# A two-layer hybrid trunk on one core: input projection, convolution taps and attention scores in another order

## The chip, the core and the metric

The kernel runs on one core of a Trainium2 chip. The metric is the time of one execution on the device in microseconds (us). The engines are named as in the profile: PE is the matrix engine (TensorE), DVE the vector engine, ACT the scalar engine, POOL GpSimd, and SP the engine from whose queue the weights are loaded. Every engine runs its own instructions in order; semaphores join them.

## What is computed

Two layers over x of 256 tokens by 1024 channels in float32. In each layer one input projection feeds a convolution module and a sparse attention, whose results are joined by one output projection; then comes a dense SwiGLU (layer 0) or a top-2-of-8 expert SwiGLU (layer 1).

```python
for layer in range(DEPTH):
    h = rms_norm(x, attn_norm_g[layer])
    z = h @ w_in[layer]
    c_val, c_gate, q, k_c, v_c, k_s, v_s, k_w, v_w, g_log = jnp.split(z, offsets, axis=-1)
    conv_out = conv_module(c_val, c_gate, ...)      # GLU, causal 31-tap depthwise conv, norm of 64 channels, silu
    attn_out = nsa_attention(q, k_c, v_c, ...)
    x = x + jnp.concatenate([conv_out, attn_out], axis=-1) @ w_out[layer]
    h = rms_norm(x, ffn_norm_g[layer])
    x = x + (swiglu(h, ...) if layer % 2 == 0 else moe_swiglu(h, ...))
```

The attention has 8 query heads of 64 in 2 key/value heads. Queries and keys are normalised per head. The compressed branch attends to 15 blocks of 32 keys, each put through a small two-layer network (cmp_k_w1, cmp_v_w1 and so on); the selected and the window branch attend, at 256 tokens, to all keys before the query under a causal mask. Three gates per head weigh the branches.

## The kernel before

**Storage.** Weights come into one ring of four slots of 2 MB (`stream` sets the order, SP loads them, and a load waits on `last_read` of what stood in its slot). In the dense and expert stages the same ring is cut into seven pieces of 1 MB. Activations of the attention live in `arena`, `hn` and `mixT`. PSUM has eight banks. The profile calls `arena` what the code calls z, qT, kT, u, y, probsT and more, so lines tell them apart.

**The stretch ahead of the attention,** in each layer. PE multiplies the normalised, transposed input `hT` with: `z_product(0, i)` (keys and values of the compressed branch and others, 512 columns, for two token tiles i), four gated chunks c (`glu(c)`, 128 channels of value and gate each, from weight chunks `win` 0 and 1), then the compression products of keys and values (L1137, weights `cmp` 0 and 1), `z_product(1, i)` (queries) and `z_product(2, i)` (keys and values of the window branch and the gate logits), with small transposes between them. DVE applies the 31 taps (`conv_taps`, L737 for the first tap and L741 for the others, one instruction per tap and chunk): first chunks 0 and 1, then 2 and 3. A chunk pair can begin when both `glu` of it are there. Between the taps DVE squares, sums and normalises queries and keys (L776 to L821) and finishes their transposes (L827, L831). The order of taps and the rest is written out by hand (`TAP_A`, `TAP_B`, `TAP_C`); the last 12 taps of chunks 2 and 3, 24 instructions, stand behind `masked_scores(1)`.

**The attention core.** There are 12 units of scores (4 heads by 128 keys for the first token tile, 2 heads by 256 keys for the second). For unit n: PE `score(n)` (L1186) writes bank n % 2; DVE adds the causal mask into `hn` (L841) and takes the negated maximum (L843); ACT exponentiates per head (L516); DVE divides by the sum and multiplies by the gate (L882 to L886); PE transposes (`transpose_probs`, L1212); ACT copies the result (L540); after the last unit of a group of heads PE multiplies with the values (`values`, L1223 and L1227). In the loop PE issues score(n+2), which waits until DVE has read unit n (`s_ready`), then the transposes of unit n. Ahead of the loop stand score(0), score(1), the compressed scores (L1200, 16 products of 15 columns), their softmax on DVE (L855 to L873) behind the last taps, and the transposes of it (L1235), whose copies by ACT (L531) PE waits for. The means and variances of the convolution (L1247, L1253) are multiplied in the loop at n = 1 and n = 5. Then follows the output projection (L1268).

**The dense stage.** For group g of 256 hidden channels (11 groups): `up` (L1288 to L1290) for w1 and w3, `down(g - 1)` (L1304 to L1306). All operands are split in a high and a low part in fp32r. `dact_hi` (ACT, L583) and `dact_lo` (DVE, L918) hold the activation of one group: writing group g - 1 waits for the products of group g - 2.

## Time and profile before

| | us |
|---|---|
| median of 3 runs | 1653.21 (1651.16 to 1655.38) |
| the profiled execution | 1654.8 |
| span of its core | 1652.8 |
| PE busy | 1563.0 (95%) |
| DVE busy | 1211.1 (73%) |
| ACT busy | 911.5 (55%) |
| mean granted clock of PE | 0.957 |

The profile's page has busy shares in 40 slices of 41.3 us, the chain of work that ended last, and the costliest groups of instructions. A row of the chain is: start, duration, engine, what it writes, line. A row of the timeline is: start, duration, engine, line, operation, out<-in, shapes, count, and in brackets how long the engine sat idle before it and who ended that. A busy PE is not PE at its peak. A float32 matmul or its weight load appears twice in the timeline of PE for one product of the program, a transpose and an fp32r matmul once.

### The profile page before, as it was taken

How to read it: one execution, taken by the hardware profiler on the slowest of the kernel's cores; microseconds unless marked ns; L12 is line 12 of the kernel's file. 1: busy time of each engine (PE TensorE's matmuls, PEld its weight loads, DVE VectorE, ACT ScalarE, POOL GpSimd, SP SyncE). 2: the span in 40 equal slices, each digit the busy share in tenths (PEclk: the TensorE clock that was granted, in tenths of full speed). 3: DMA queues.
4: the chain of work that ended last, by engine and by line, in shares of the span. 5: the costliest groups of instructions: out<-in, count | busy, mean ns of one | idle time of the engine just before them, and what ended most of it. 6: DMA issues, size and time to landing. Idle time of an engine off the chain costs nothing.

```text
span 1652.8 us, 19780 instructions
## 1 busy us (share of the span) xinstructions
PE 1563.0 (95%) x7336; PEld 1233.4 (75%) x7336; DVE 1211.1 (73%) x1186; ACT 911.5 (55%) x834; POOL 24.3 (1%) x41
## 2 busy tenths in 40 slices
PE   6968899998896888999999999999999999999998
PEld 4654389998665437888888888888888888888886
DVE  2876254453287624888987988987988987989896
ACT  1024233432102424677777777777777677777674
POOL 1010000000001000000000000000000000000000
PEclk9977899999997788999999999999999999999999
DMA  8500086541551003999999999999999998999992
GB/s 291 180 2 1 0 286 205 189 161 53 202 181 51 1 0 136 356 367 371 361 359 332 365 368 371 361 359 334 361 371 372 360 365 328 359 372 365 363 364 102
DMA packets 199396, 426.57 MB, mean 258 GB/s; under 512 B 7314, under 2 KB 40338, under 8 KB 199316
## 3 DMA queue, kind: packets, MB, share of 16 engines
q1 hardware_dynamic: 198000, 424.89, 71.4%
q8 instruction: 64, 1.05, 0.3%
q10 hardware_dynamic: 1316, 0.49, 0.1%
q14 instruction: 16, 0.13, 0.0%
HBM read 424.31 MB, written 1.05 MB: 257 GB/s over the span
## 4 chain that ended last, share of the span: by engine, by line
PE 89%; DVE 7%; issue 2%; ACT 2%; DMA 1%; ACTq 0%; POOL 0%; POOLq 0%; DVEq 0%
PE bank L1387 13%; PE bank L1389 12%; PE bank L1388 12%; PE bank L1094 8%; PE bank L1411 6%; PE bank L1409 6%; PE bank L1410 6%; PE bank L1290 3%; PE bank L1289 3%; PE bank L1288 3%; PE bank L1268 3%; PE bank L1227 2%; PE bank L1137 2%; PE bank L1397 1%; PE bank L1186 1%
## 5 line engine op out<-in xcount | busy, mean ns | idle before, releaser
L717 DVE TENSOR_TENSOR w_lo<-ring,w_hi 128x2048 fp32r<-128x2048 f32 x369 | 843.1, 2291 | 184.3 <-ACT w_hi L471 183.8
L471 ACT CAST w_hi<-ring 128x2048 fp32r<-128x2048 f32 x369 | 705.4, 1914 | 268.3 <-PE bank L1389 165.3
L1387 PE MATMUL bank<-w_hi,xe_hi 128*128 128x512 f32 x896 | 355.2, 396 | 7.4 <-DVE w_lo L717 7.4
L1389 PE MATMUL bank<-w_hi,xe_lo 128*128 128x512 f32 x896 | 350.1, 391 | 0.0
L1388 PE MATMUL bank<-w_lo,xe_hi 128*128 128x512 f32 x896 | 349.7, 390 | 0.0
L1387 PEld LDWEIGHTS bank<-w_hi,xe_hi 128*128 128x128 f32 x896 | 168.7, 188 | 43.0 <-DVE w_lo L717 9.6
L1389 PEld LDWEIGHTS bank<-w_hi,xe_lo 128*128 128x128 f32 x896 | 168.6, 188 | 35.9
L1388 PEld LDWEIGHTS bank<-w_lo,xe_hi 128*128 128x128 f32 x896 | 168.9, 188 | 33.2
L1409 PE MATMUL bank<-w_hi,actT_hi 128*128 128x512 f32 x448 | 175.1, 391 | 0.0
L1410 PE MATMUL bank<-w_lo,actT_hi 128*128 128x512 f32 x448 | 174.5, 389 | 0.0
L1411 PE MATMUL bank<-w_hi,actT_lo 128*128 128x512 f32 x448 | 174.4, 389 | 0.0
L1288 PE MATMUL bank<-hT_hi,w_hi 128*128 128x256 f32 x352 | 99.6, 283 | 0.0
L1290 PE MATMUL bank<-hT_hi,w_lo 128*128 128x256 f32 x352 | 99.6, 283 | 0.0
L1289 PE MATMUL bank<-hT_lo,w_hi 128*128 128x256 f32 x352 | 99.6, 283 | 0.0
L1411 PEld LDWEIGHTS bank<-w_hi,actT_lo 128*128 128x128 f32 x448 | 84.1, 188 | 17.6
L1409 PEld LDWEIGHTS bank<-w_hi,actT_hi 128*128 128x128 f32 x448 | 84.1, 188 | 17.0
L1410 PEld LDWEIGHTS bank<-w_lo,actT_hi 128*128 128x128 f32 x448 | 84.1, 188 | 17.0
L741 DVE SCALAR_TENSOR_TENSOR arena<-arena,par 128x256 f32<-128x256 f32 x240 | 96.1, 477 | 0.0
L712 DVE TENSOR_TENSOR x_sb<-x_sb,bank 128x512 f32<-128x512 f32 x48 | 30.6, 683 | 67.9 <-PE bank L1268 58.7
L1094 PE MATMUL bank<-ring,hT 128*128 128x512 f32 (+1 forms) x192 | 74.4, 543 | 3.2 <-DVE hT L705 3.2
L1289 PEld LDWEIGHTS bank<-hT_lo,w_hi 128*128 128x128 f32 x352 | 67.5, 192 | 0.4
L1288 PEld LDWEIGHTS bank<-hT_hi,w_hi 128*128 128x128 f32 x352 | 67.5, 192 | 0.4
(224 smaller groups left out, 1472.7 us busy)
## 6 DMA issues: line engine op xcount, KB each, us to landing
ring<-in_moe_w SPq DMA_DIRECT2D x336, 1024.0 KB, 6.1
ring<-in_dense_w SPq DMA_DIRECT2D x33, 1024.0 KB, 5.4
ring<-in_w_in SPq DMA_DIRECT2D x8, 2048.0 KB, 10.3
ring<-in_w_out SPq DMA_DIRECT2D x4, 2048.0 KB, 9.0
ring<-in_cmp_k_w SPq DMA_DIRECT2D x2, 2048.0 KB, 19.2
ring<-in_cmp_v_w SPq DMA_DIRECT2D x2, 2048.0 KB, 8.7
ring<-in_w_in SPq DMA_DIRECT2D x2, 1120.0 KB, 11.4
x_sb<-in_x SPq DMA_DIRECT2D x2, 512.0 KB, 5.1
```

The costliest lines, as they stand in the source:

```text
L471: nc.scalar.copy(w_hi[t % SPLIT][:], raw(t)).then_inc(w_hi_ready, 1)
L717: V.tensor_tensor(w_lo[t % SPLIT][:], raw(t), w_hi[t % SPLIT][:].bitcast(F32), ALU.subtract).then_inc(w_lo_ready, 1)
L1094: last = T.matmul(dst, lhs(k), rhs(k), start=(n == 0), stop=(n == len(chunks) - 1))
L1288: T.matmul(dst, hi[:, k, c], hT_hi[:, k, :], start=(k == 0), stop=False)
L1289: T.matmul(dst, hi[:, k, c], hT_lo[:, k, :], start=False, stop=False)
L1290: last = T.matmul(dst, lo[:, k, c], hT_hi[:, k, :], start=False, stop=(k == KD - 1))
L1387: T.matmul(dst, xe_hi[:, kk, own], hi[:, k, :], start=(kk == 0), stop=False)
L1388: T.matmul(dst, xe_hi[:, kk, own], lo[:, k, :], start=False, stop=False)
L1389: last = T.matmul(dst, xe_lo[:, kk, own], hi[:, k, :], start=False, stop=(kk == KD - 1))
L1409: T.matmul(dst, actT_hi[:, c % 2, f], hi[:, k, r], start=first, stop=False)
L1410: T.matmul(dst, actT_hi[:, c % 2, f], lo[:, k, r], start=False, stop=False)
L1411: last = T.matmul(dst, actT_lo[:, c % 2, f], hi[:, k, r], start=False, stop=end)
```

## The change

1. Loads: `win` 0 and 1 come first and in halves of 256 columns. The first halves of both (chunks 0 and 1) signal `glu_arrived[0]`, the second halves `glu_arrived[1]`. `win` 3 comes third. The load of the compression weights of the values now takes over the slot of `win` 0 and waits for the fourth gated chunk.
2. PE makes chunks 0 and 1 first, then `z_product(0, i)`, chunk 2, the transposes for the compression, chunk 3.
3. DVE's taps are placed anew: all 124 stand ahead of the first `masked_scores`.
4. Queries and keys are normalised, transposed and finished per token tile, one part earlier; kT is transposed in two parts.
5. The compressed keys `kcT` are laid out block-diagonally (zeroed at the start by GpSimd), so that 8 products of 64 columns replace 16 of 15, in one bank, ahead of the last key transposes. Their softmax takes fewer, wider instructions. It stands on DVE between `masked_scores(0)` and `masked_scores(1)` and behind the first unit's probabilities; its transposes come at n = 1 of the loop and not ahead of it.
6. The causal mask enters the bank by one fp32r matmul (`ident_r` by `causal_r`, 512 columns) ahead of each unit's scores, which accumulate on it. DVE's add (L841) is gone; the maximum and ACT's exponentials read PSUM. Score(n+2) now waits for unit n's exponentials (`exp_ready`).
7. `dact_hi` and `dact_lo` have two buffers.
8. The means of the convolution are multiplied at n = 2.

DVE around the first scores of a layer. Before:

```order
L741 SCALAR_TENSOR_TENSOR arena<-arena,par 128x256 x6
L821 TENSOR_TENSOR hn<-arena,rstat 128x128 x2
L827 TENSOR_SCALAR arena<-bank0,par 128x4x128
L827 TENSOR_SCALAR arena<-bank1,par 128x4x128
L831 TENSOR_SCALAR arena<-bank2,par 128x256 x2
L841 TENSOR_TENSOR hn<-bank0,causal 128x512
L843 TENSOR_REDUCE negmax<-hn 128x4
L841 TENSOR_TENSOR hn<-bank1,causal 128x512
L843 TENSOR_REDUCE negmax<-hn 128x4
L741 SCALAR_TENSOR_TENSOR arena<-arena,par 128x256 x24
L855 TENSOR_TENSOR cp<-bank6,cneg 128x4x15 x2
```

The same place of the changed kernel, where L757 are the taps, L814 and L819 finish queries and keys, L866 is the maximum, and L908 the first unit's probabilities:

```order
L814 TENSOR_SCALAR arena<-bank7,par 128x4x128
L847 TENSOR_TENSOR arena<-arena 128x128 x2
L848 TENSOR_REDUCE stat<-arena 128x4
L849 TENSOR_SCALAR stat<-stat 128x4
L814 TENSOR_SCALAR arena<-bank5,par 128x4x128
L819 TENSOR_SCALAR arena<-bank2,par 128x256
L854 TENSOR_TENSOR hn<-arena,rstat 128x128 x2
L757 SCALAR_TENSOR_TENSOR arena<-arena,par 128x256 x4
L819 TENSOR_SCALAR arena<-bank3,par 128x256
L866 TENSOR_REDUCE negmax<-bank0 128x4
L875 TENSOR_TENSOR cp<-bank6,cneg 128x16x15
L876 TENSOR_REDUCE cmx<-cp 128x16
```

No tap stands between the first scores and the compressed softmax any more, and four stand shortly before the first scores.

PE from the first score of a layer to the loop. Before, with the transposes of the compressed probabilities (L1235) ahead of the third unit's scores:

```order
L1186 MATMUL bank0<-arena 128x128 x4
L1186 MATMUL bank1<-arena 128x128 x4
L1200 MATMUL bank6<-kcT,arena 128x15 x8
L1200 MATMUL bank7<-kcT,arena 128x15 x8
L1235 MATMUL bank6<-ident,cp 64x128 x4
L1235 MATMUL bank7<-ident,cp 64x128 x4
L1186 MATMUL bank0<-arena 128x128 x4
L1212 MATMUL bank2<-ident,hn 128x128 x4
L1186 MATMUL bank1<-arena 128x128 x4
L1212 MATMUL bank3<-ident,hn 128x128 x4
```

Now (L1217 compressed scores, L1228 mask, L1232 scores, L1249 transposes of probabilities, L1273 those of the compressed ones):

```order
L1217 MATMUL bank6<-kcT,arena 128x64 x8
L1199 MATMUL bank3<-ident,hn 128x128 x2
L1228 MATMUL bank0<-causal_r,ident_r 128x512
L1232 MATMUL bank0<-arena 128x128 x4
L1228 MATMUL bank1<-causal_r,ident_r 128x512
L1232 MATMUL bank1<-arena 128x128 x4
L1228 MATMUL bank0<-causal_r,ident_r 128x512
L1232 MATMUL bank0<-arena 128x128 x4
L1249 MATMUL bank2<-ident,hn 128x128 x4
L1228 MATMUL bank1<-causal_r,ident_r 128x512
L1232 MATMUL bank1<-arena 128x128 x4
L1249 MATMUL bank3<-ident,hn 128x128 x4
```

The compressed scores moved ahead of the first scores, and their transposes (L1273, the next rows) behind the second unit's.

The loads that SP issues for layer 0, before:

```order
L347 DMA ring<-in_w_in 128x8x512 x3
L347 DMA ring<-in_cmp_k_w 128x16x256
L347 DMA ring<-in_cmp_v_w 128x16x256 [waits z_psum]
L347 DMA ring<-in_w_in 128x8x512 [waits glu_psum]
L347 DMA ring<-in_w_in 128x8x280 [waits glu_psum]
```

And now:

```order
L353 DMA ring<-in_w_in 128x8x256 x2
L356 DMA ring<-in_w_in 128x8x256 x2
L359 DMA ring<-in_w_in 128x8x512
L359 DMA ring<-in_cmp_k_w 128x16x256
L359 DMA ring<-in_cmp_v_w 128x16x256 [waits glu_psum]
L359 DMA ring<-in_w_in 128x8x512 [waits glu_psum]
```

The load of `cmp_v_w` moved from behind `z_product(0)` to behind the last gated chunk.

The core of the diff:

```diff
-        stream += [("win", l, 3), ("win", l, 0), ("win", l, 1), ("cmp", l, 0), ("cmp", l, 1), ("win", l, 2), ("win", l, 4)]
+        stream += [("win", l, 0), ("win", l, 1), ("win", l, 3), ("cmp", l, 0), ("cmp", l, 1), ("win", l, 2), ("win", l, 4)]
...
-                sp.dma_start(dst[:, 0:k * m].rearrange("p (k n) -> p k n", k=k), src).then_inc(arrived, 16)
+                dst = dst[:, 0:k * m].rearrange("p (k n) -> p k n", k=k)
+                if key in halved:
+                    sp.dma_start(dst[:, :, 0:S], src[:, :, 0:S]).then_inc(glu_arrived[0], 16)
+                    if key[2] == 1:
+                        for c in range(2):
+                            sp.dma_start(view("win", key[1], c)[:, :, S:BANK],
+                                         source("win", key[1], c)[0][:, :, S:BANK]).then_inc(glu_arrived[1], 16)
+                else:
+                    sp.dma_start(dst, src).then_inc(arrived, 16)
...
-                            if g >= 2:
-                                sc.wait_ge(w_used, piece_of["d2", 0, g - 2] + 1)
-                            nc.scalar.copy(dact_hi[:].rearrange("p a t -> p (a t)"),
+                            if g >= 3:
+                                sc.wait_ge(w_used, piece_of["d2", 0, g - 3] + 1)
+                            nc.scalar.copy(dact_hi[:, (g - 1) % 2].rearrange("p a t -> p (a t)"),
...
                 link(V.memset(blkT[:], 0.0))
+                glu(0)
+                glu(1)
+                dv.wait_ge(u_ready, CC * l + 2)
+                conv_taps(0, range(16))
                 for i in range(NT):
                     dv.wait_ge(z_ready, 6 * l + i + 1)
...
-                glu(0)
+                conv_taps(0, range(16, 23))
+                glu(2)
...
-                glu(1)
-                dv.wait_ge(u_ready, CC * l + 2)
-                conv_taps(0, range(6))
-                glu(2)
-                conv_taps(0, range(6, 15))
+                conv_taps(0, range(23, TAPS))
                 glu(3)
-                conv_taps(0, range(15, TAPS))
...
-                conv_taps(2, range(TAP_A))
+                conv_taps(2, range(22))
                 square_sums_q(0)
-                conv_taps(2, range(TAP_A, TAP_B))
+                conv_taps(2, range(22, 26))
+                normalised_q(0)
...
-                    s3 = scores[:, n % 2, :].rearrange("p (h k) -> p h k", h=nh)
-                    link(V.tensor_tensor(s3, bank[n % 2][:].rearrange("p (h k) -> p h k", h=nh),
-                                         causal[:, 2 * P - keys:].unsqueeze(1).to_broadcast([P, nh, keys]), ALU.add))
-                    V.tensor_reduce(negmax[:, n % 2, 0:nh], s3, AX_X, ALU.max, negate=True).then_inc(s_ready, 1)
+                    V.tensor_reduce(negmax[:, n % 2, 0:nh], bank[n % 2][:].rearrange("p (h k) -> p h k", h=nh),
+                                    AX_X, ALU.max, negate=True).then_inc(s_ready, 1)
...
                 masked_scores(0)
+                compressed_scores()
                 masked_scores(1)
-                conv_taps(2, range(TAP_C, TAPS))
...
+                    if n == 0:
+                        compressed_probs()
-                    if n == 2:
+                    if n == 3:
...
                     if n >= 2:
-                        pe.wait_ge(s_ready, NU * l + n - 1)
+                        pe.wait_ge(exp_ready, exp_count(l, n - 2))
                     r = slice(kv * HD, (kv + 1) * HD)
+                    T.matmul(bank[n % 2][:], ident_r[:],
+                             causal_r[:, 2 * P - keys:].unsqueeze(1).to_broadcast([P, nh, keys]),
+                             start=True, stop=False)
                     for h in range(nh):
                         last = T.matmul(bank[n % 2][:, h * keys:(h + 1) * keys], qT[r, h0 + h, i * P:(i + 1) * P],
-                                        kT[r, b, 0:keys], start=True, stop=True)
+                                        kT[r, b, 0:keys], start=False, stop=(h == nh - 1))
```

## Rows read from the trace of the kernel before

**Rows 1.** The page: granted clock in 40 slices, in tenths, then the chain's engines.
```profile
PEclk9977899999997788999999999999999999999999
PE 89%; DVE 7%; issue 2%; ACT 2%; DMA 1%; ACTq 0%; POOL 0%; POOLq 0%; DVEq 0%
```

**Rows 2.** Chain of waits, layer 0's attention core, from the first scores on.
```profile
105.67 3.79 PE bank L1186 x16
...
110.90 9.50 DVE arena L741 x24
...
125.17 1.93 PE bank L1235 x8
127.13 1.07 ACT arena L531 x2
128.24 2.07 PE bank L1186 x8
...
141.68 1.07 PE bank L1186 x4
```

**Rows 3.** Chain of waits, layer 1: first scores, output projection.
```profile
518.54 3.79 PE bank L1186 x16
...
599.20 13.95 PE bank L1268 x32
```

**Rows 4.** Windows: busy and count by engine, granted clock, DMA share, GB/s; in the core.
```profile
112.00:116.00 4.00, 3.26 (x20) 3.15 (x18) 4.00 (x12) 0.58 (x4) 0.00 (x0) 0.50 0.01 2
152.00:156.00 4.00, 4.00 (x16) 2.15 (x15) 3.79 (x9) 2.37 (x8) 0.00 (x0) 1.00 0.00 0
180.00:184.00 4.00, 4.00 (x6) 0.98 (x5) 0.00 (x0) 2.44 (x5) 0.00 (x0) 0.50 0.00 0
```

**Rows 5.** Timeline of the stretch ahead: compression products, then DVE's wait for queries.
```profile
67.79 7.11 PE L1137 MATMUL bank<-ring,arena 128*47 128x256 f32 x32
83.17 0.69 DVE L776 TENSOR_TENSOR arena<-arena 128x512 f32<-128x512 f32 x1 [0.25 <-ACT arena L482]
99.75 1.09 PE L1170 MATMUL bank<-ident,hn 128*128 128x128 f32 x8 [0.48 <-ACT arena L482]
```

**Rows 6.** The page: one load, its size, us from issue to landing.
```profile
ring<-in_cmp_v_w SPq DMA_DIRECT2D x2, 2048.0 KB, 8.7
```

**Rows 7.** Timeline of the core: one unit's pieces, and values at either clock.
```profile
130.24 1.12 PE L1212 MATMUL bank<-ident,hn 128*128 128x128 f32 x4
137.21 0.69 DVE L892 TENSOR_TENSOR arena<-arena,bank 128x512 f32<-128x512 f32 x1 [0.37 <-PE bank L1247]
139.75 1.93 PE L1227 MATMUL bank<-arena 128*64 128x512 f32 x4
164.58 6.58 PE L1227 MATMUL bank<-arena 128*64 128x512 f32 x8
186.14 27.73 PE L1268 MATMUL bank<-ring,mixT 128*128 128x512 f32 x64
```

**Rows 8.** Groups by line and shape over 0 to 225 us: busy, mean ns.
```profile
L843 DVE TENSOR_REDUCE negmax<-hn 128x4 f32<-128x512 f32 x4 | 2.7, 686 | 0.1
L516 ACT ACTIVATE hn<-hn,negmax 128x256 f32<-128x256 f32 x16 | 8.0, 500 | 3.1 <-DVE negmax L843 3.0
```

**Rows 9.** Chain of waits in the expert stage: fp32r matmuls of 512 columns.
```profile
661.47 0.43 PE bank L1387
...
662.25 0.23 PE bank L1389
```

**Rows 10.** Timeline of the end of the dense stage.
```profile
401.49 0.69 DVE L927 TENSOR_TENSOR dact<-dsg,bank 128x512 f32<-128x512 f32 x1 [6.78 <-PE bank L1290]
...
406.94 0.62 ACT L583 CAST dact_hi<-dact 128x512 fp32r<-128x512 f32 x1 [10.68 <-PE bank L1306]
411.73 0.79 PE L1304 MATMUL bank<-w_hi,dact_hi 128*128 128x512 f32 x1 [4.89 <-DVE w_lo L717]
```

**Rows 11.** A window in which PE ran transposes alone (L1086, L1075).
```profile
427.00:428.00 1.00, 1.00 (x12) 1.00 (x11) 1.00 (x2) 0.00 (x0) 0.00 (x0) 1.00 1.09 345
```

More of the change, by code:

```diff
@@ L78, in hymba_trunk @@
     slot_of = {key: n for n, key in enumerate(slots)}
+    halved = [key for key in slots if key[0] == "win" and key[2] < 2]
+    turn_of = {key: len([o for o in slots[:n + 1] if o not in halved and slot_of[o] % SLOTS == n % SLOTS])
+               for n, key in enumerate(slots)}
     piece_of = {key: n for n, key in enumerate(pieces)}
@@ L207, in hymba_trunk @@
         x_loaded, par_loaded = sem("x_loaded"), sem("par_loaded")
+        glu_arrived = [sem(f"glu{h}_arrived") for h in range(2)]
         slot_arrived = [sem(f"slot{s}_arrived") for s in range(SLOTS)]
@@ L1192, in _ @@
                 score(1)
-                pe.wait_ge(kcT_ready, l + 1)
-                pe.wait_ge(vc_ready, l + 1)
-                for kv in range(KV):
-                    r = slice(kv * HD, (kv + 1) * HD)
-                    for i in range(NT):
-                        for g in range(G):
-                            o = (i * G + g) * CPAD
-                            last = T.matmul(bank[6 + kv][:, o:o + NCMP], qT[r, g, i * P:(i + 1) * P],
-                                            kcT[r, kv * CPAD:kv * CPAD + NCMP], start=True, stop=True)
-                    last.then_inc(cs_psum, 1)
                 def transpose_probs(n):
@@ L1303, in down @@
                                     dst, r = bank[2 * n + i][:], slice(i * P, (i + 1) * P)
[L1304 to L1306 removed]
+                                    T.matmul(dst, dact_hi[:, g % 2, f, r], hi[:, f, c], start=first, stop=False)
+                                    T.matmul(dst, dact_hi[:, g % 2, f, r], lo[:, f, c], start=False, stop=False)
+                                    last = T.matmul(dst, dact_lo[:, g % 2, f, r], hi[:, f, c], start=False, stop=end)
                         last.then_inc(w_used, 1)
```

204 lines of the change are left out of this document (116 added, 88 removed).

## The prediction

> **What bounds the kernel now.** I read the page first. PE stands for 89% of the chain and its clock is granted in full in most of the 40 slices; it drops in three places, slices 3 to 4, slice 10 and slices 13 to 15 [rows 1]. Those are the attention core of layer 0, the end of the dense stage and the core of layer 1. Between them PE works without a gap worth naming, and nothing that the change touches runs in the expert stage after about 650 us. So the chain of waits is read next, in those places only.
>
> In layer 0 the first scores start at 105.67 and the output projection at 186.14 [rows 2, 7]: a core of 80.5 us. In layer 1 it is 518.54 to 599.20, 80.7 us, with the same pieces [rows 3]. In both, PE has made two units of scores and the compressed scores and then waits for DVE, which works through 24 taps (9.5 us) and the compressed softmax: PE's next instruction, the transposes at 125.17, comes ten microseconds after its last [rows 2]. After that the loop of 12 units alternates between a full clock and half of it: 1.00 at 152 to 156, 0.50 at 112 to 116 and at 180 to 184 [rows 4]. Four value products cost 1.93 at the one and eight cost 6.58 at the other, 0.46 against 0.82 each [rows 7]. The third place is one wait: the last `down` of the dense stage starts 4.89 us late, because ACT could only write `dact_hi` once PE had read the last one [rows 10].
>
> **Part 1: the stretch ahead of the scores.** The products are the same, in another order, and PE stays the bound if DVE keeps up. From the first gated pair (about 31) to the scores (106) DVE has 74 us. Its work there is 124 taps at 9.50/24 = 0.40 [rows 2], 49 us, and some 18 us of other steps that it had before: 67. The closest point is the squares of the queries, for which DVE waited 0.25 us before [rows 5]. With the new order, laid one step after the other behind their gated chunks (glu 0 and 1 by 32; 30 taps and two first taps to 45; 14 to 52; the compression input 4 us; 16 to 64; 44 to 81.5) DVE is there at 81.5, and the queries come at about 84. So 2.8 us of cover; beyond that every microsecond would count.
>
> Two things are added on PE's path. The load of the compression weights of the values is issued only when chunk 3 is done, at 60.2, and takes 8.7 us [rows 6]; PE wants them at 67.79 [rows 5], so it waits 60.25 + 8.7 - 67.8 = 1.1. And four transposes of queries (half of the 1.09 for eight [rows 5]) now stand ahead of the last projection product: 0.55. Behind that product, the way to the first score took 105.67 - 99.75 = 5.9 [rows 2, 5]. Of it two taps go (0.8) and one 512-column finish (0.7), since one token tile's queries are done earlier; one more round between PE and DVE for the second half of the keys costs some 0.3: 4.7. The compressed scores fit into PE's wait there. Sum: 1.1 + 0.55 - 1.2 = +0.4 for each layer. At the start of layer 0 the halved loads bring rows of 1 KB; even at the 2 MB in 8.7 us of rows 6 the first 2 MB land ahead of 16 us, when PE starts. Bounds of this part: -0.5 (no wait for the load) to +3 (load 2 us later, DVE's cover used up).
>
> **Part 2: the core up to the fourth unit.** Before: first score to the head of n = 3 (the score at 141.6), 35.9 us [rows 2]. Now, with a unit's scores at 1.07 (8 instructions at half clock: 2.07) [rows 2], and the mask's matmul, which the trace before does not have in this place: its nearest row is an fp32r matmul of 512 columns, 0.23 at full clock, 0.43 at half [rows 9]. At full clock: units 0 and 1 until 2.6; maximum 0.72 [rows 8] and four exponentials 2.3, until 4.5; score(2) and the transposes of unit 0 until 6.5. ACT does unit 1 until 6.8 and the compressed exponential until 7.3; DVE the compressed rest (2.2), the maximum of unit 2 (0.7) and the probabilities of unit 1 (1.1) until 11.4; PE its transposes (0.6) and the compressed ones (1.1) until 13.1; two copies by ACT as in rows 2, until 14.4; score(4), transposes (0.59, half of the 1.12 at low clock [rows 7]), means (4 instructions of 512 columns, 1.75) and values (6 of them, 2.65, by the 0.46 of rows 7 or a little less) until 20.7. At half clock the same list ends at about 30; half clock up to the means and full behind gives 26.5. PE has holes of 2 to 3 us here, so I take the clock low until unit 3, nearly: 25.5. The gain is 35.9 - 25.5 = 10.4: the 9.5 us of taps, moved under the projections, and about one more.
>
> **Part 3: units 3 to 11.** Before: 186.14 - 141.6 = 44.5. PE's work at full clock now: 7 scores at 1.07 + 0.23 = 9.1, 9 transposes at 0.59 = 5.3, variances 1.75, values 2.65 + 2 x 4.35 = 11.35: 27.5. Its waits: the mask's 0.7 on DVE is gone from each unit, but score(n+2) now comes behind unit n's exponentials (two at 0.50 + 0.1 each [rows 8], 1.35), side by side with DVE's probabilities (1.1). Where values stand in between this hides; in the last four units it does not, and following exponential, score, maximum, exponential I get 7.1 us of waits. That makes 34.6 at full clock throughout. With the last value products at half clock, as at 180 to 184, +4.4; with those of the third group too, another +4. I take 39: the holes of over a microsecond ahead of the last values are still there. The same list for the units before, with the clock of its rows, comes out some 2 us long, which is within this choice. Gain 44.5 - 39 = 5.5. ACT reading PSUM instead of SBUF I cost at nothing, bounds -1.5 to +1.5 for the core.
>
> A core then takes 64.5 instead of 80.5. The Trainium skill (TensorE: Matmul & The Clock Gate, Part 4) says that transposes don't count as busy for the clock. By that the clock would stay low here. The trace disagrees: at 427 to 428 only transposes ran and the granted clock was 1.00, after 0.50 before them [rows 11].
>
> **Part 4: the dense stage.** From the start of `dact_hi` to PE's start it was 411.73 - 406.94 = 4.8, the splitting of the last weights by ACT and DVE. With two buffers `dact_hi` can be written when DVE's product is there, at 402.2 [rows 10]: PE starts at 402.2 + 4.8 + 0.2 = 407.2 instead of 411.73, -4.5. After the wait of 4.9 the clock was at half for the first ten matmuls or so, 0.43 instead of 0.23 [rows 9]; with a wait of 0.6 that should go, -2.2, bounds 0 and -2.4. In the other groups PE did not wait, so nothing changes there.
>
> **Sum.** Two layers x (0.4 - 10.4 - 5.5) = -31.0; dense -6.7; together -37.7. 1654.8 - 37.7 = 1617.1 against the profiled execution, which is 1.6 above the median: **1615.5**. The copies of the mask and the clearing of kcT lie in the first 7 us, when ACT and GpSimd wait for x.
>
> **The rivals.**
> (a) The clock stays at full speed in the core, because the mask's matmuls fill PE: 20.7 + 34.6 = 55.3 per core, 9.2 less each: 1615.5 - 18.4 = 1597. For it: each unit has more columns than before; against it: PE still stands still for 2 to 3 us at four places.
> (b) DVE or the load decides ahead of the scores: the cover of 2.8 us is gone and the load comes 2 us later; +2.6 per layer, +5: about 1621. For it: DVE is now busy for 67 of 74 us.
> (c) The lost lookahead costs more: score(n+2) behind the exponentials serialises every unit, also those that I let hide behind values. 1.3 us for 7 units and the third value group at half clock, 10 less 3 of it already counted, so +6 per core: about 1628.
> (d) Slower than before: the clock stays at half through the whole core, as it did from 104 to 136. PE's list at half clock is 77 us of work, with waits 83.5, and the output projection, which began at full clock, loses 2. Per layer 83.5 + 0.4 + 2 - 80.5 = +5.4, two layers 10.8, dense only -4.5: +6.3, 1659.5. It decides from a core of over 82 us. Against it: the full clock came back three times in the old loop, with less work in it. The rule of the Trainium skill that is named above points here.
> (e) The change doesn't do what it says: the taps do fill the time ahead, but PE then waits there as long as it did behind; the gain of part 2 is nil. That is 1636. DVE's idle time in the stretch ahead speaks against it.
>
> **Chances.** Forecast (1608 to 1619) 50%; (a) 13%; (b) 16%; (c) 13%; (d) 3%; (e) 5%. The range leaves out the lower half of (a), (d) and (e): 1602 to 1630. About 0.3%, 5 us, is what a measurement can tell from no change. Faster 0.95, the same 0.02, slower 0.03.
>
> **What would show it.** In the profile after: no taps behind the first maximum; the first scores of layer 0 at 105 to 107; from there to the output projection 60 to 69 us; a wait of about a microsecond at the second compression product; the last `down` of the dense stage less than a microsecond behind the one before, at full clock; the distance from the output projection of layer 1 to the end as before. A core of under 58 us makes (a) right, one over 70 (c). If the expert stage itself gets longer or shorter, the sum was made in the wrong place.

## The result, and the profile after

| | us |
|---|---|
| before, median of 20 runs | 1654.48 (1650.40 to 1656.76) |
| changed kernel, median of 20 runs | 1642.07 (1634.67 to 1658.54) |
| ratio | 0.9928, 95% interval 0.9915 to 0.9942 |
| profiled execution after: span | 1641.6 |
| the same, PE busy, clock | 1586.6 (97%), 0.97 |

The change gains 12 us, not the 38 that were predicted, and the time lies above the predicted range. The sign was right, the size was not.

The page after, busy time of the engines, then the granted clock in 40 slices (the counterpart of [rows 1]):

```profile
PE 1586.6 (97%) x7328; PEld 1227.3 (75%) x7328; DVE 1194.1 (73%) x1156; ACT 908.1 (55%) x834; POOL 24.0 (1%) x42
...
PEclk9978999999997799999999999999999999999999
```

The clock's two drops below 9 are shorter, two slices each instead of three and four. (The prediction counted three drops and named slice 10; [rows 1] has a 9 there. The clock does fall at the end of the dense stage, to 0.50 at 412 to 416, but too briefly to bring that slice below 9.) But PE is busy for 23.6 us more than before (1563.0) in a kernel that is shorter and in which its waits shrank. That is the first sign that its work got slower somewhere.

The chain of waits after, start and duration, from layer 0 to the first expert product; it answers to [rows 2, 3]. L1228 is the first mask, L1309 the output projection, L1428 the first expert product:

```profile
59.03 8.37 DMA ring<-in_cmp_v_w
67.44 7.11 PE bank L1163 x32
...
104.53 0.76 PE bank L1228
...
130.58 0.43 PE bank L1228
...
170.81 19.51 PE bank L1309 x45
```
```profile
395.57 1.29 DVE x_sb L729 x2
449.43 9.29 DMA ring<-in_cmp_v_w
458.77 8.79 PE bank L1163 x32
...
497.77 0.76 PE bank L1228
565.24 13.95 PE bank L1309 x32
623.36 0.80 PE bank L1428
```

In the kernel before, the last dense products ended at 419.63 and the expert products began at 658.57:

```profile
419.63 0.69 DVE x_sb L712
...
658.57 0.77 PE bank L1387
```

Laid side by side, every difference has a place:

| stretch | before | after | difference | predicted |
|---|---|---|---|---|
| start to the first scores, layer 0 | 105.67 | 104.53 | -1.1 | +0.4 |
| core, layer 0 | 80.5 | 66.3 | -14.2 | -15.9 |
| output projection to the end of the dense stage | 233.5 | 224.8 | -8.7 | -6.7 |
| from there to the first scores of layer 1 | 98.9 | 102.2 | +3.3 | +0.4 |
| core, layer 1 | 80.7 | 67.5 | -13.2 | -15.9 |
| output projection to the first expert product | 59.4 | 58.1 | -1.3 | 0 |
| expert stage | 994.2 | 1018.2 | +24.0 | 0 |

Up to the expert stage the changed kernel is 35.2 us ahead (37.7 predicted). Then it loses 24 in a stage in which no instruction was changed. Two windows of 25 us in it, before and after, columns as in [rows 4]; PE does nothing but matmuls of 512 columns in both, with no idle time and at a granted clock of 1.00:

```profile
733.00:758.00 25.00, 25.00 (x114) 20.71 (x113) 22.41 (x14) 18.28 (x12) 0.00 (x0) 1.00 1.02 374
```
```profile
733.00:758.00 25.00, 25.00 (x111) 20.14 (x110) 22.28 (x15) 19.14 (x16) 0.00 (x0) 1.00 1.01 365
```

114 matmuls against 111 in the same time, those under way at the edges counted. The timeline of PE shows the pace of one, if one takes starts and not durations (the matmuls overlap). Before, six starts lie 1.36 us apart, 0.227 each; after, 1.40, 0.233:

```profile
733.00 0.39 PE L1388 MATMUL bank<-w_lo,xe_hi 128*128 128x512 f32 x1
...
734.36 0.39 PE L1388 MATMUL bank<-w_lo,xe_hi 128*128 128x512 f32 x1
```
```profile
732.85 0.39 PE L1428 MATMUL bank<-w_hi,xe_hi 128*128 128x512 f32 x1
...
734.25 0.39 PE L1428 MATMUL bank<-w_hi,xe_hi 128*128 128x512 f32 x1
```

Over the whole stage the mean from start to start is 0.2272 before and 0.2332 after. There are 4032 such matmuls: 4032 x 0.0060 = 24 us, all of the loss. The page says it in one row for each kernel (mean duration 396 against 402 ns), and its idle time has not grown, so nothing is waited for:

```profile
L1387 PE MATMUL bank<-w_hi,xe_hi 128*128 128x512 f32 x896 | 355.2, 396 | 7.4 <-DVE w_lo L717 7.4
```
```profile
L1428 PE MATMUL bank<-w_hi,xe_hi 128*128 128x512 f32 x896 | 360.6, 402 | 6.8 <-DVE w_lo L734 6.8
```

### The profile page after: what moved, and what is told of

The parts are those of the page before. It is cut to its first block, busy times and chain, and to the rows that moved or that the text cites. A ratio compares the mean times of both kernels' runs of the same rounds, so it can differ in the third digit from the quotient of the medians.

```text
span 1641.6 us, 19740 instructions
## 1 busy us (share of the span) xinstructions
PE 1586.6 (97%) x7328; PEld 1227.3 (75%) x7328; DVE 1194.1 (73%) x1156; ACT 908.1 (55%) x834; POOL 24.0 (1%) x42
## 4 chain that ended last, share of the span: by engine, by line
PE 91%; DVE 4%; issue 2%; ACT 2%; DMA 1%; POOL 0%; ACTq 0%; POOLq 0%; DVEq 0%; SPq 0%
PE bank L1428 13%; PE bank L1430 13%; PE bank L1429 13%; PE bank L1120 8%; PE bank L1450 6%; PE bank L1452 6%; PE bank L1451 6%; PE bank L1309 3%; PE bank L1329 3%; PE bank L1331 3%; PE bank L1330 2%; PE bank L1264 2%; PE bank L1438 1%; PE bank L1345 1%; PE bank L1347 1%
## 5 line engine op out<-in xcount | busy, mean ns | idle before, releaser
L1428 PE MATMUL bank<-w_hi,xe_hi 128*128 128x512 f32 x896 | 360.6, 402 | 6.8 <-DVE w_lo L734 6.8
L1429 PE MATMUL bank<-w_lo,xe_hi 128*128 128x512 f32 x896 | 355.0, 396 | 0.0
L1430 PE MATMUL bank<-w_hi,xe_lo 128*128 128x512 f32 x896 | 354.9, 396 | 0.0
L1428 PEld LDWEIGHTS bank<-w_hi,xe_hi 128*128 128x128 f32 x896 | 169.0, 189 | 46.6 <-DVE w_lo L734 8.4
L757 DVE SCALAR_TENSOR_TENSOR arena<-arena,par 128x256 f32<-128x256 f32 x240 | 96.2, 480 | 0.1
```

The source lines that it names most:

```text
L1428: T.matmul(dst, xe_hi[:, kk, own], hi[:, k, :], start=(kk == 0), stop=False)
L1429: T.matmul(dst, xe_hi[:, kk, own], lo[:, k, :], start=False, stop=False)
L1430: last = T.matmul(dst, xe_lo[:, kk, own], hi[:, k, :], start=False, stop=(kk == KD - 1))
```

## What made the expert stage slower

**The theory.** Three tensors of the change stand in SBUF ahead of the activations of the dense and the expert stage: `kcT` grew from 47 to 64 columns (64 bytes more per partition, with the rounding of its place), `ident_r` (512 bytes) and `causal_r` (1024 bytes) are new. So the room of the attention's `mixT` and `arena`, and with it `hT_hi`, `dact_hi`, `xe_hi`, `actT_hi`, which use the same room later, moved by 1600 bytes, while the weights `w_hi` and `w_lo` stand ahead of all of them and stayed. Theory A: the pace of a matmul depends on where its operands lie. (The operand that is loaded into PE is called stationary, in the expert products the activations; the other, there the weights, is streamed through and called moving.) Rivals: the new instructions leave something behind that slows PE, or the loads or the copies by ACT and DVE, which now fall at other moments, collide with it.

**e1 and e2** move the activations of the kernel before and change nothing else, by an unused tensor behind `vc`: 400 columns (1600 bytes) and 16 (64 bytes).

```diff
+        gap = sb("gap", [P, 400])     # e2: 16, e3: 32
```

> The kernel before, with an unused tensor of 1600 bytes per partition ahead of the activation areas, so that these stand where they stand in the changed kernel; no instruction changes. The changed kernel reached the output projection of layer 1 some 33 us earlier than before, but its expert stage took 22.8 us longer (1017 against 994 us), with fp32r matmuls 0.2334 us apart instead of 0.2278 on average. Theory A (placement: the pace of the matmuls depends on where the stationary operands stand): this kernel is slower than before by 20 to 25 us, all of it in the expert stage, with 0.233 us between matmuls. Theory B (the earlier start or another order of events brings the loads or the engines into another rhythm): the same time as before within 3 us and 0.228 us.

> The kernel before with the activation areas shifted by 64 bytes per partition only. Theory A1 (placement, and what counts is whether an area starts at a multiple of 128 bytes): 20 to 25 us slower than before, as with a shift of 1600. Theory A2 (placement, but the distance of 1600 bytes or the crossing of a larger boundary counts): the same as before within 3 us. Theory B: the same as before within 3 us.

> The kernel before with the activation areas shifted by 128 bytes. Theory A1: the same as before within 3 us. Theory A2 leaves it open: between 0 and +23 us. Theory B: the same as before within 3 us.

> The changed kernel with the activation areas shifted by another 64 bytes, to a multiple of 128. Theory A1: the expert stage goes back to about 994 us and the time to 1619 us, 34 us under before. Theory A2: 1642 us, as the changed kernel. Theory B: 1642 us.

Measured: e1 1676.31 us, ratio to before 1.0124 (1.0101 to 1.0147); e2 1676.83, 1.0127 (1.0106 to 1.0148). Both have 0.2332 us for each expert matmul. An empty tensor alone costs the kernel before 20 to 21 us: the new instructions, the loads and the waits are out, and 64 bytes do what 1600 do (1600 = 6 x 256 + 64). The loss lies where it lay in the changed kernel, in the expert stage: 1016.6 us in both traces against 994.2 before. The page's row of e2:

```profile
L1387 PE MATMUL bank<-w_hi,xe_hi 128*128 128x512 f32 x896 | 360.0, 402 | 6.4 <-DVE w_lo L717 6.4
```

e3 (128 bytes) took 1673.74, 1.0109 (1.0086 to 1.0132), with 0.2324, and e4, the changed kernel with 64 bytes more, 1639.52, 0.9897 (0.9857 to 0.9937), with 0.2325. So 128 bytes are no better a place than 64, or hardly. The idea that any multiple of 128 would do fell.

**e5** moves the two areas of the changed kernel on until they are 2048 bytes from where they stood before, **e6** places the expert stage's two groups apart: `h_hi` to `xe_lo` at 128 modulo 512, `actT_hi` and what follows at 384. (`w_hi` is placed at byte 82048 of each partition, which is 128 modulo 512; `xe_hi` at 187776 before, 189376 in the changed kernel and 189824 in e5, so 0, 64 and 0 from it modulo 256.) **e7** moves weights and activations of the kernel before together by 64 bytes.

```diff
-        hT_hi, hT_lo = sb_d("hT_hi", [P, KD, S], F32R), sb_d("hT_lo", [P, KD, S], F32R)
+        gap_d = sb_d("gap_d", [P, 112]); hT_hi, hT_lo = sb_d("hT_hi", [P, KD, S], F32R), sb_d("hT_lo", [P, KD, S], F32R)
...
-        h_hi, h_lo = sb_e("h_hi", [P, NT, D], F32R), sb_e("h_lo", [P, NT, D], F32R)
+        gap_e = sb_e("gap_e", [P, 112]); h_hi, h_lo = sb_e("h_hi", [P, NT, D], F32R), sb_e("h_lo", [P, NT, D], F32R)
```

> The changed kernel with 448 unused bytes ahead of the activations of the dense stage and of those of the expert stage, so that both start 2048 bytes behind their place in the kernel before, at the same place within 512 bytes (384). So far, by the place within 512 bytes: 384 gave 0.2272 us between fp32r matmuls of 512 columns, 448 gave 0.2332, 0 gave 0.2324. Theory A3 (the pace goes by the place of the stationary operands within 512 bytes or a part of them): 0.2272 in the expert stage, which takes 994 us again, and 1619 us in all. Theory A4 (the kernel before stood at the one good distance from the weights by chance): 0.232 to 0.233 and 1640 us.

> The changed kernel with the gathered inputs of the experts (stationary in L1428 to L1430) at 128 within 512 bytes and their hidden activations (stationary in L1450 to L1452) at 384. Theory A3: the second group is paced at 0.2272; the first too if only the place within 256 bytes counts, 0.232 to 0.233 if it is within 512. Theory A4: both at 0.232 to 0.233. The time follows: 1619, 1634 or 1640 us, as two thirds of the matmuls are of the first group.

> The kernel before with 64 unused bytes behind the raw weights: the split weights, which move, and the stationary activations both stand 64 bytes further, their distance unchanged. If the distance of the two operands sets the pace: 0.2272 and the time of before within 3 us. If the place of the stationary operand alone does: 0.2332 and 20 us slower than before, as with 64 bytes ahead of the activations only.

e5: **1619.93 us**, ratio 0.9795 (0.9773 to 0.9818), 22.1 less than the changed kernel. Its row, again with 396 ns:

```profile
L1428 PE MATMUL bank<-w_hi,xe_hi 128*128 128x512 f32 x896 | 355.0, 396 | 7.8 <-DVE w_lo L734 7.8
```

e6: 1619.49, 0.9781 (0.9750 to 0.9812), both groups at 0.2273, while its dense stage, left where the change had put it, kept 0.2333. So the places repeat every 256 bytes, each product goes by its own operands, and nothing is left behind from one stage to the next. e7: 1654.47, 0.9997 (0.9984 to 1.0009), at 0.2273: with both operands moved, nothing happens. It is the distance between them that counts, not the place.

One rival is left: ACT and DVE write the weights that PE reads, so the distance could set how they collide with PE. A stretch in which neither of them works rules it out. At the end of the dense stage, first before, then after:

```profile
417.00:419.00 2.00, 2.00 (x11) 1.63 (x10) 0.00 (x0) 0.00 (x0) 0.00 (x0) 1.00 1.05 393
```
```profile
390.00:395.00 5.00, 5.00 (x23) 4.04 (x22) 0.00 (x0) 0.00 (x0) 0.00 (x0) 1.00 0.88 277
```

The 512-column products start 0.228 apart in the first (417.15 to 419.20, nine steps) and 0.233 in the second (390.95 to 395.15, 18 steps). The loads, which go on there, write into `ring`; e2 and e7 move the activations equally far from it, and only e2 is slower. So the cause of the loss is the distance of PE's two operands; why it acts so, no run shows.

## What the parts of the change are worth

From here the kernel with the repaired layout (e5) is the base, so that the core can be measured without the expert stage. Only the dense part was done alone, on the kernel before.

**e8**: two buffers for `dact_hi` and `dact_lo`, nothing else.

> The kernel before with the two buffers of the dense activations alone; nothing moves within 512 bytes. The step of the prediction: PE starts the last down 4.5 us earlier and at full clock, 6.7 us less, 1648 against 1655. Rival: the wait goes but the gain is lost behind it, since the next layer's weights or the additions to x come last: 0 to 3 us.

1645.64 us, 0.9945 (0.9925 to 0.9964): -9 us, with an interval of 6 to 12, where 6.7 was predicted. In the trace the dense stage, from the output projection on, takes 226.63 us and not 233.45: -6.8. The rival (0 to 3 us) fell. DVE's last steps of the dense stage in e8, then PE's first `down` behind them. Against [rows 10] the wait of 4.89 is gone, the first matmul starts at 406.32 instead of 411.73, and none runs at 0.43:

```profile
400.78 0.69 DVE L927 TENSOR_TENSOR dact<-dsg,bank 128x512 f32<-128x512 f32 x1 [7.30 <-PE bank L1290]
...
403.97 2.29 DVE L717 TENSOR_TENSOR w_lo<-ring,w_hi 128x2048 fp32r<-128x2048 f32 x1 [1.12 <-ACT w_hi L471]
```
```profile
406.32 0.50 PE bank L1304
406.82 0.23 PE bank L1305
```

**e9** puts 24 taps back behind the second unit's maximum, **e10** puts the mask and the wait of score(n+2) back on DVE, **e11** loads the compression weights of the values into the slot of `win` 3, which is free earlier, **e12** is e11 with `hT_hi` and `hT_lo` at 64 modulo 256 from the weights and `dact_hi`, `dact_lo` at 0. These four ran on one chip and e5 on another, so they are best compared by their ratios to the kernel before, which ran beside each.

```diff
-                conv_taps(2, range(22))
+                conv_taps(2, range(19))
...
                 masked_scores(1)
+                conv_taps(2, range(19, TAPS))
```
```diff
-                        pe.wait_ge(exp_ready, exp_count(l, n - 2))
+                        pe.wait_ge(s_ready, NU * l + n - 1)
...
-                    T.matmul(bank[n % 2][:], ident_r[:],
-                             causal_r[:, 2 * P - keys:].unsqueeze(1).to_broadcast([P, nh, keys]),
-                             start=True, stop=False)
...
+                    link(V.tensor_tensor(s3, bank[n % 2][:].rearrange("p (h k) -> p h k", h=nh),
+                                         causal[:, 2 * P - keys:].unsqueeze(1).to_broadcast([P, nh, keys]), ALU.add))
```
```diff
+    for l in range(L):
+        n = slot_of["win", l, 0]
+        slot_of["cmp", l, 1], slot_of["win", l, 2], slot_of["win", l, 4] = n + 6, n + 4, n + 5
+        slot_of["wout", l, 1] = n + 10
```
```diff
+        gap_d = sb_d("gap_d", [P, 48])
         dact_hi, dact_lo = sb_d("dact_hi", [P, 2, 2, S], F32R), sb_d("dact_lo", [P, 2, 2, S], F32R)
```

> The changed kernel with the repaired layout of e5 (1619.9 us), and in it one part of the change undone: the last 12 taps of chunks 2 and 3 (24 instructions) stand behind the second unit's maximum again, as in the kernel before. The prediction put the gain of their place at 9.5 of the 10.4 us of part 2 in each layer. Theory A (part 2 as told): DVE reaches the first unit's probabilities 24 x 0.40 = 9.5 us later and PE, which stands at their transposes, waits as long; a little comes back ahead of the scores, where four taps stood (0.8 per layer): +17 us, 1637. Rival B (PE had holes that the taps fill in part, and the new order of the compressed softmax hides some): +10 or less, 1630 or below. Rival C (rival (e) of the prediction, PE only waits elsewhere): no difference, 1620.

> The changed kernel with the repaired layout of e5 (1619.9 us), and in it the mask undone: DVE adds it into SBUF and takes the maximum there, the exponentials read SBUF, PE's 12 mask products per layer are gone, and score(n+2) waits for the maximum of unit n and no longer for its exponentials. Theory A (part 3 as told, the mask's addition gone from each unit weighs more than the lookahead): 0.69 us per unit come back on the path for 10 of 12 units, less the lookahead's gain, so +3 to +5 us per layer, +8 in all: 1628. Rival B (rival (c) of the prediction, the lost lookahead costs as much as the addition saved): no difference, 1618 to 1622. Rival C (the lookahead is worth more): faster by 4 us or more, 1616 or below.

> The changed kernel with the repaired layout of e5 (1619.9 us), and in it the compression weights of the values are loaded into the slot of win 3, which is free after z_product(0), and win 2 and win 4 into those of win 0 and win 1; the order of the loads stays. The load of the values' weights no longer waits for the fourth gated chunk. The trace of e5 shows PE waiting 0.82 us for this load in layer 0 and 2.15 us in layer 1, where the products behind it also run at a lower clock. Theory A (the added wait of part 1 is all that it costs, and the clock falls because of it): both waits go, with 1 to 2 us of slow products in layer 1: -4 to -5 us, 1615.5. Rival B (the clock falls in layer 1 for another reason): -3 us, 1617. Rival C (the load is late because the ring's transfers are, not because of its wait): no difference.

> e11, and with it the dense stage's operands placed apart: hT_hi and hT_lo (the 256-column operands of the products with w1 and w3) at 64 bytes modulo 256 from w_hi, dact_hi and dact_lo (the stationary operands of the 512-column products) at 0. The 256-column products took 0.1178 us at the distance of 64 and 0.1199 at 0, the 512-column ones 0.2333 and 0.2279. Theory A (each group of products goes by its own distance): 0.1178 and 0.228, so 1056 x 0.0021 = 2.2 us less than e11: 1613.3. Rival B (the two were coupled in another way): one of the two paces does not follow, and the time is that of e11 or more.

| | us | ratio to before (95%) |
|---|---|---|
| e5, base | 1619.93 | 0.9795 (0.9773 to 0.9818) |
| e9, taps back | 1628.59 | 0.9834 (0.9808 to 0.9861) |
| e10, mask back | 1622.08 | 0.9810 (0.9793 to 0.9827) |
| e11, load freed | 1612.67 | 0.9742 (0.9714 to 0.9771) |
| e12, and dense places | **1609.69** | 0.9726 (0.9709 to 0.9744) |

e9: 8.7 us above e5 by the medians, 6.5 by the ratios: rival B. Its trace says otherwise, which e13 and e14 take up.

e10: 2.1 us above e5 by the medians, 2.5 by the ratios, with an interval of some 5 us to either side. The mask on PE instead of DVE can't be told from nothing, and theory A (8 us) fell. e10 puts back the mask and the earlier lookahead together, so it shows that the two cancel, as rival (c) has it for this term, and not the size of either.

e11: the load's waits were priced at 1.1 us in each layer. In the changed kernel PE waits 0.85 us in layer 0 and 1.78 in layer 1, and in layer 1 the clock falls with it: the products behind the wait took 8.79 and not 7.11 (the chain above, 67.44 and 458.77). Windows of layer 1 around it, of the changed kernel and of e11:

```profile
456.00:460.00 4.00, 2.22 (x8) 0.79 (x6) 4.00 (x12) 0.38 (x1) 0.00 (x0) 0.85 1.07 378
460.00:464.00 4.00, 4.00 (x15) 2.06 (x14) 4.00 (x12) 0.00 (x0) 0.00 (x0) 0.72 1.07 376
```
```profile
456.00:460.00 4.00, 4.00 (x21) 2.27 (x19) 4.00 (x12) 0.00 (x0) 0.00 (x0) 1.00 1.08 377
460.00:464.00 4.00, 4.00 (x16) 1.84 (x15) 4.00 (x12) 0.38 (x1) 0.00 (x0) 1.00 0.83 302
```

The fall of the clock doesn't come in every execution: in those of e5 and e13 the products behind waits of 2.15 and 1.84 us took 7.11 (the expectation of e11 has it otherwise for e5, wrongly), and so they did in e6, e9, e14 and e16 behind 1.8 to 2.0 us; in that of e15 (1.86) they took 8.79 again, and in e4 8.79 and 8.62 behind 2.40 and 2.01. The waits are 2.6 to 3.0 us together, the slow products 1.7 where they come. The medians of e11 and e5 are 7.3 us apart (8.8 by the ratios, 3 to 15 with their intervals), more than theory A's 4 to 5. The traces don't show where more would come from: they are 1.1 us apart (e5's is its fastest execution), the first scores of layer 0 come 0.8 earlier, and of the 2.15 in layer 1 only 0.9 comes through, since the products ahead of the wait start 1.6 later behind the dense stage. That the load costs more than its waits rests on the medians alone.

e12: 3.0 less than e11 (2.2 expected; alone within the noise). The paces are what was aimed at, 0.1178 for the 256-column products and 0.2282 for the 512-column ones. It beats both kernels: 2.7% less than before, 2.0% less than the change as it stood. Rival B, that one pace doesn't follow, fell.

**e13 and e14** repeat e5 and e9 side by side, since e9's trace showed both cores 8.8 us longer, 17.6 together, and its median only 8.7.

> The kernel of e5 once more (the changed kernel with both activation areas moved back into step), beside the next one on the same chip, as the measure for it. Theories A and B both: 1620, within 1614 to 1622; the two cores at 66.5 and 64 us in the profiled execution.

> The kernel of e9 once more (24 taps behind the second unit's maximum), measured directly against e13. In e9's profiled execution both cores were 8.8 us longer than in e5's, +17.6 us together, while the median was only 8.7 us above e5's and the profiled execution was the slowest of four (1622.9 to 1634.9). Theory A (the taps are worth what the trace of one execution shows, and the first median was low by chance): a median 14 to 19 us above e13. Theory B (in most executions the clock in the core rises earlier or the waits are shorter than in the one that was profiled, so the taps are worth half): 6 to 10 us above e13, and in a profiled execution near the median the cores are only 3 to 5 us longer each.

e13 1621.15 (1619.73 to 1627.91), 0.980 (0.978 to 0.982); e14 1629.62 (1625.40 to 1634.61), 0.986 (0.9838 to 0.9882). The difference is 8.5 us again (9.9 by the ratios, 5 to either side), so theory B: the taps alone are worth some 8.5 for two layers, not 19. What theory B said of the traces missed: the two cores take 142.7 us together in e13's, its slowest execution, and 138.3 in e14's, its fastest. The second traces also show why one trace misled. e5 and e13 are the same program, and the core of layer 0, measured as in the table above, takes 66.5 us in the one and 75.9 in the other. In both the clock falls to half about the first scores; in e5 it is back by 126, in e13 only at 143.5. Windows of e5, then of e13:

```profile
120.00:128.00 8.00, 8.00 (x17) 2.98 (x15) 3.01 (x6) 0.59 (x1) 1.64 (x1) 0.64 0.00 0
128.00:136.00 8.00, 8.00 (x28) 3.65 (x27) 3.24 (x8) 4.18 (x13) 0.25 (x1) 1.00 0.00 0
```
```profile
128.00:136.00 8.00, 8.00 (x16) 3.64 (x15) 1.62 (x4) 2.60 (x9) 0.35 (x1) 0.50 0.00 0
136.00:144.00 8.00, 8.00 (x15) 2.40 (x13) 1.62 (x4) 1.18 (x4) 0.00 (x0) 0.53 0.00 0
144.00:152.00 8.00, 7.94 (x34) 4.79 (x34) 5.88 (x11) 4.94 (x16) 0.00 (x0) 1.00 0.01 2
```

PE is busy without a hole in both from 120 on, and its holes of 116 to 120 are alike (1.2 us each); the moment at which the clock comes back is not set by the program alone. One profile of a core here is good to some 9 us.

**e15 and e16.** The cores got 27 us shorter in the traces, the taps carry 8.5 and the mask 1 to 2 if anything. e15 puts the compressed softmax and its transposes back where the kernel before has them, e16 does that and puts the taps back too.

```diff
                 masked_scores(0)
-                compressed_scores()
                 masked_scores(1)
+                compressed_scores()
+                compressed_probs()
...
+                transpose_cp()
                 for n in range(NU):
                     if n + 2 < NU:
                         score(n + 2)
                     transpose_probs(n)
-                    if n == 1:
-                        transpose_cp()
```

> The kernel of e13 (changed kernel, both activation areas moved back into step, 1621.2 us), and in it the compressed softmax and its transposes where the kernel before has them: DVE does the whole softmax behind the second unit's maximum and ahead of the first unit's probabilities, PE transposes it ahead of the third unit's scores, ACT copies it there. The taps stay ahead. Theory A (this place is on the path: DVE's softmax 3.3 us, 1.91 us of transposes and 1.06 of copies at its end, less the 1.1 us by which PE waited for those copies at their new place): 5 us per layer, +10: 1631. Rival B (the shorter chain also lets the clock rise earlier, so its place is worth more than its own length): +16 or more, 1637. Rival C (hidden beside the first units): within 3 us, 1624 or below.

> e15, and with it the 24 taps behind the second unit's maximum (e14 alone: +8.5 us), so that DVE's order around the first scores is that of the kernel before. Theory A (the two add up, the delays stand in a row on DVE): the sum of e14's and e15's differences, by the expectation for e15 8.5 + 10: 1640. Rival B (the taps on the path count with their full 9.5 us per layer once nothing else of DVE's can be done beside them, as part 2 of the prediction had it): 19 above e15, 1650. Rival C (less than the sum, since one hole of PE holds both): within 4 us of the larger of the two.

e15 1629.02 (1624.27 to 1629.84), 0.9837 (0.9822 to 0.9853); e16 1649.19 (1647.58 to 1654.03), 0.9973 (0.9960 to 0.9986). Against e13: the softmax alone +7.9, the taps alone +8.5, both **+28.0** (by the ratios 6.1, 9.9 and 28.6, each with 4 to 5 us to either side). With the softmax in its old place the taps cost 20.2 us, which is the 19 that part 2 had, and rival B of e16. They don't add up, they reinforce; theory A, the sum of the two, fell. The chain of layer 0 shows the two delays in a row in e16, from the first mask to the output projection:

```profile
104.54 0.77 PE bank L1225
...
110.77 9.50 DVE arena L757 x24
...
124.19 1.93 PE bank L1270 x8
126.14 1.07 ACT arena L548 x2
...
144.59 0.43 PE bank L1225
...
184.96 27.68 PE bank L1305 x64
```

and the same place in e14, where only the taps are back:

```profile
111.06 9.51 DVE arena L757 x24
...
125.35 1.12 PE bank L1247 x4
126.47 1.72 PE bank L1271 x8
...
136.05 0.42 PE bank L1226
```

The timeline shows how long PE stood still before it went on, in e16 and then in e14:

```profile
124.19 1.91 PE L1270 MATMUL bank<-ident,cp 128*64 128x128 f32 x8 [14.15 <-DVE cp L889]
```
```profile
121.64 1.12 PE L1247 MATMUL bank<-ident,hn 128*128 128x128 f32 x4 [8.58 <-DVE hn L906]
```

PE goes on 2.5 us later in e16, but the fourth unit's head is reached at 144.6 there and at 136.1 in e14, 8.5 later. In e16 the scores of the third and fourth unit and the first unit's transposes still lie ahead at 127.25, since they stand behind the softmax's transposes on PE; in e14 they are done by 125.4, the third unit's scores before PE stood still, while DVE worked at the taps. The other part is the clock, which is full from about 128.5 on in e14 and from about 142 in e16. What of the 28 is order and what is the moment of the clock's return these runs don't separate. With both undone, e16's cores take 80.4 and 79.8 us in the trace, as long as those of the kernel before (80.5 and 80.7), although its mask is still on PE.

## Why the prediction was wrong

**The step that failed** is the sentence in the opening, on what bounds the kernel, that nothing the change touches runs in the expert stage. The change touches its addresses. Everything else in the sum was asked of instructions, waits and queues, and no step asked where the new tensors stand. The prediction's last line named the sign by which this would show, the expert stage getting longer, and it did: +24.0 in the trace, 22 by e5. In its place the runs showed that the new tensors moved the activations by 64 bytes modulo 256 against the weights, which costs 0.0060 us for each of 4032 expert products. With the layout repaired the same change gives 1619.9 to 1621.2, inside the predicted range and 4 to 6 us above the forecast of 1615.5.

**Part 1** (+0.4 per layer): -1.1 in layer 0 and +3.3 in layer 1. The wait for the load was there, as told, 0.85 and 1.78 us against 1.1 (0.62 to 2.40 over the traces of all runs that have it). The miss is in layer 1: the wait is longer there, and in this execution the clock fell behind it and cost 1.7 us of slow products. This was not in the sum. DVE's cover held: it waited 2.50 us for the queries' squares (2.8 predicted; 0.25 before [rows 5]), so rival (b) is wrong for DVE and half right for the load, which came up to 1.3 us later than priced and not 2:

```profile
82.82 0.69 DVE L792 TENSOR_TENSOR arena<-arena 128x512 f32<-128x512 f32 x1 [2.50 <-ACT arena L498]
```

**Part 2** (first score to the fourth unit's head 25.5): 130.58 - 104.53 = 26.1. The total was right and its explanation too narrow: "the 9.5 us of taps and about one more" gives the taps nearly all of it, but alone they are worth 4.3 per layer and the softmax's new place 4.0, and only both together 14, which is more than this part's whole gain and about that of parts 2 and 3 together. A part that hangs on a chain with two delays in it cannot be priced by the one that is longer.

**Part 3** (units 3 to 11 in 39): 170.81 - 130.58 = 40.2, 1.2 off, and the layers' cores of 66.3 and 67.5 against 64.5. Rival (a), full clock throughout, and (d), half clock throughout, are both out: the clock is at half from 104 until nearly 128 and full afterwards, but for two stretches around the last values, 148 to 155 and 162 to 169. The size was right and its cause was not: the gain was put on the mask's 0.7 us of DVE for each unit, less the wait for the exponentials, and e10 shows nothing left of the two together, while e16, with the mask on PE and the taps and the softmax back, has cores as long as before. So the gain of part 3 hangs on the two delays of part 2 as well. That the sum of parts 2 and 3 came out near is in part luck.

**Part 4** (-6.7): -9 by the medians of e8 and -6.8 in its trace. In the trace after it is -8.7, of which 1.8 is the dense stage's changed pace (with the old places, in e5, that stage takes 226.6 and not 224.8). Mechanism, place and size were right.

**The rule of the Trainium skill** in rival (d) (TensorE: Matmul & The Clock Gate, Part 4) would have kept the clock low in the core. It came back in every trace. Since scores and values run between the transposes here, the cores by themselves don't decide it; the place of [rows 11] does. PE had stood still for 4.17 us there and then, from 423.76 to 429.67, ran nothing but transposes: at a granted clock of 0.50 from 424 to 426 and of 1.00 from 427 on. So the clock rose while only transposes ran, against the rule.

**The account** in medians: 1654.5 - 9 (dense) - 28 (taps and softmax together) - 1.5 (mask) + 22 (pace) = 1638, against 1642.1 measured. With the 6.8 of the traces for the dense stage it is 1640. The 2 to 4 us that are left would fit the load's waits and their clock (2.6 and 1.7 us in the trace after), but the terms are known to some 4 us each.

## What to carry to other kernels

A new or grown tensor moves every tensor behind it: before a stage is called untouched, list its operands' addresses before and after, and if a pace changes with no wait, count instructions in two equal windows. Move an operand area by an empty tensor of 64 bytes to see whether its place matters, and then place it on purpose. When two delays stand in one chain, undo each alone and both together: the single ones told 8 and 8, the pair 28. And one trace is not enough where the clock is on its way up.

## What the runs showed of the hardware

- The pace of an fp32r matmul depends on the distance in SBUF between its stationary and its moving operand, modulo 256 bytes. With 512 moving columns, start to start at a granted clock of 1.00: 0.2272 us at 0 (before, e5 to e7), 0.2332 at 64 (after, e1, e2), 0.2324 at 128 (e3, e4). Distances other than multiples of 64 and a distance of 192 were not tried.
- With 256 moving columns it goes the other way: 0.1199 to 0.1200 at 0, 0.1178 at 64 (0.1171 in the trace after), 0.1187 and 0.1198 at 128 (e3, e4). The best place differs by stage (e12).
- The place of the operands by itself does not count (e7), nor does a distance of 256 against 512 (e6).
- Behind waits of 1.78 us (the trace after) and 1.86 (e15) in layer 1 the granted clock fell, and 32 products took 8.79 us instead of 7.11 (after: 0.85 and 0.72 in two windows of 4 us); behind one of 2.15 us in e5 it did not. Of eleven such waits of 1.78 to 2.40 us, over all traces, the clock fell behind four.
- Two executions of one program (e5 and e13) got the full clock back at about 126 and at about 143.5 us, with PE equally busy up to 126 and without a hole from 120 on in both.
- PE stood still for 4.17 us and then ran transposes alone; the granted clock was 0.50 at first, 0.74 in the window 426 to 427 and 1.00 in the next ([rows 11]).
